# Expert stage of a diffusion step: down weights held in the array, one ring of weight halves, context rows in quarters

## What is computed

```python
aff = softmax(ht @ w_router)              # per request group
gates, idx = top_k(aff.T, cap)            # cap = 128 latent, 32 context
xs = ht[idx]
a = einsum('ecd,edf->ecf', xs, w_gate)    # 16 experts, d = 1024, f = 2816
u = einsum('ecd,edf->ecf', xs, w_up)
y = einsum('ecf,efd->ecd', silu(a) * u, w_down) * gates[..., None]
out = zeros.at[idx].add(y)                # x = x + gate2 * out
```

## Time and profile before

| | us |
|---|---|
| median of three runs | 3479.28 |
| span of the profiled execution | 3480.6 |
| first gate matmul of expert 0 starts | 883.12 |
| last down matmuls of expert 15 start | 3430.77 |
| PE busy | 3166.9 |
| DVE busy | 2532.4 |
| POOL busy | 1483.4 |
| ACT busy | 1278.2 |

### The profile page before, as it was taken

How to read it: one execution, slowest core, us unless ns; L and a number is a source line. 1 busy time by engine, 2 the same in 40 slices (tenths; PEclk the granted TensorE clock), 3 DMA queues, 4 the chain that set the end, 5 groups by cost and what they waited for, 6 DMA issues and landing times. The chain is left out here.

```text
span 3480.6 us, 50738 instructions
## 1 busy us (share of the span) xinstructions
PE 3166.9 (91%) x19191; PEld 2741.1 (79%) x19191; DVE 2532.4 (73%) x3014; ACT 1278.2 (37%) x2046; POOL 1483.4 (43%) x860
## 2 busy tenths in 40 slices
PE   8999989894899999989898999999898989999994
PEld 2699987683788888878787888888787878888883
DVE  2343331225789898988898898989898989889895
ACT  2222221232334434434343344343434343434432
POOL 2233330123345455453545454544535354535443
PEclk9999999996899999999999999999999999999997
DMA  7311102344667676776767676767667576767673
GB/s 303 114 37 36 38 14 74 117 147 151 205 220 247 210 233 214 223 223 212 238 211 240 221 231 217 236 215 234 220 210 245 195 255 205 245 224 226 218 237 134
DMA packets 483305, 668.23 MB, mean 192 GB/s; under 512 B 14689, under 2 KB 418993, under 8 KB 480050
## 3 DMA queue, kind: packets, MB, share of 16 engines
q1 hardware_dynamic: 476978, 644.45, 55.6%
q0 software_dynamic: 6144, 20.98, 2.5%
HBM read 633.39 MB, written 31.98 MB: 191 GB/s over the span
## 5 line engine op out<-in xcount | busy, mean ns | idle before, releaser
L1202 POOL TENSOR_TENSOR wD_lo<-rawW,wD_hi 128x1024 fp32r<-128x1024 f32 x352 | 960.3, 2759 | 1162.7 <-DVE wD_hi L1541 1162.7
L1401 PE MATMUL psU<-X,wU_hi 128*128 128x320 f32 x2816 | 784.7, 360 | 93.1 <-DVE wU_lo L1202 93.1
L1401 PE MATMUL psG<-X,wG_hi 128*128 128x320 f32 x2816 | 760.9, 352 | 38.2 <-issue 35.1
L1202 DVE TENSOR_TENSOR wU_lo<-rawW,wU_hi 128x1024 fp32r<-128x1024 f32 x350 | 741.2, 2125 | 0.0
L1403 PE MATMUL psU<-X,wU_lo 128*128 128x160 f32 x2816 | 685.0, 243 | 0.0
L1403 PE MATMUL psG<-X,wG_lo 128*128 128x160 f32 x2816 | 677.7, 241 | 0.0
L1401 PEld LDWEIGHTS psU<-X,wU_hi 128*128 128x128 f32 x2816 | 552.7, 196 | 98.6 <-DVE wU_lo L1202 51.0
L1401 PEld LDWEIGHTS psG<-X,wG_hi 128*128 128x128 f32 x2816 | 543.7, 193 | 62.9 <-issue 41.7
L1403 PEld LDWEIGHTS psU<-X,wU_lo 128*128 128x128 f32 x2816 | 562.9, 200 | 0.0
L1403 PEld LDWEIGHTS psG<-X,wG_lo 128*128 128x128 f32 x2816 | 552.5, 196 | 6.4
L1202 DVE TENSOR_TENSOR wG_lo<-rawW,wG_hi 128x1024 fp32r<-128x1024 f32 x350 | 454.6, 1336 | 56.9 <-ACT wG_hi L1208 56.9
(11 more groups left out here) (239 smaller groups left out, 4213.0 us busy)
## 6 DMA issues: line engine op xcount, KB each, us to landing
rawW<-in_w_gate SPq DMA_DIRECT2D x176, 1024.0 KB, 7.4
rawW<-in_w_up SPq DMA_DIRECT2D x176, 1024.0 KB, 8.2
rawW<-in_w_down SPq DMA_DIRECT2D x176, 1024.0 KB, 4.9
wm<-in_w_mod SPq DMA_DIRECT2D x24, 1024.0 KB, 5.0
raw<-in_w_in SPq DMA_DIRECT2D x32, 192.0 KB, 2.4
rawc<-catT SPq DMA_DIRECT2D x10, 512.0 KB, 6.0
acc<-x SPq DMA_DIRECT2D x10, 512.0 KB, 2.7
xn<-xn SPq DMA_DIRECT2D x10, 512.0 KB, 4.1
```

Of the source, the lines that this page charges most:

```text
L1202: eng.tensor_tensor(lo, src, hi.bitcast(F32), ALU.subtract).then_inc(f_lo[kind], 1)
L1401: pe.matmul(out[:, f, 0:2 * C], hi, X[:, k, :], start=(k == 0), stop=False, skip_group_check=True)
```

## The change

The stage is written anew; the parts before and after it stay, but for the gate row of routing.

- **Weights.** All weights of an expert are 66 halves of 128x1024: 44 of gate and up, in the order of the steps, then 22 of down. A down half is four blocks of 128x256 out of one of four passes over the 1024 output columns. The halves run through one ring of 11 raw buffers (`RAW`) and one of 6 split buffers (`SPLIT`), whose place goes on over the change of expert. ACT makes every `hi` and DVE every `lo`, four halves ahead of PE in their lists (`AHEAD`); POOL makes none after routing.
- **Down.** It follows after the eleven gate and up steps. The weights are held and the hidden values stream, in pairs of 320 and 160 columns as for gate and up: 4 passes x 22 blocks x 2 = 176 pairs, into `psD0` and `psD1` by turns. The results are columns of tokens. ACT copies a pass's lo columns out, scaled by the gate vector (`y_low`); DVE adds the rest, scaled too (`y_sum`). Ten transposes turn all to rows (`columns_to_rows`), after the up matmuls of the next expert's first step, and ACT copies them out with the token's gate (`y_rows`).
- **Context.** Its 32 rows of 1024 are gathered and scattered as 128 rows of 256. The gathered rows are turned in one place, after the first pass (`rows_to_columns`, ten transposes); ACT and DVE modulate them (`x_modulated`).
- **Routing.** The gate row's operations go; three copies and four scalings of indices come on DVE, and two more halves to split.

The diff, cut to its core (of removed lines, only those that nothing replaces):

```diff
+        HALF = NK // 2 * W_STEP
+        GU_HALVES, HALVES = 4 * STEPS, 6 * STEPS
+        PASSES, FB = 4, FF // P
+        RAW, SPLIT, AHEAD = 11, 6, 4
+        raw = sb("rawW", [P, RAW, HALF])
+        w_hi, w_lo = sb("w_hi", [P, SPLIT, HALF], F32R), sb("w_lo", [P, SPLIT, HALF], F32R)
...
+        def parts(n):
+            if n < GU_HALVES:
+                i, kind, half = n // 4, n // 2 % 2, n % 2
+                return [((wg_, wu_)[kind], 4 * half, 4, i * W_STEP)]
+            t = 4 * (n - GU_HALVES)
+            inside = min(4, FB - t % FB)
+            out = [(wd_, t % FB, inside, t // FB * W_STEP)]
+            return out + ([(wd_, 0, 4 - inside, (t // FB + 1) * W_STEP)] if inside < 4 else [])
...
+        def load(sp, e, n):
+            at = 0
+            for src, row, rows, col in parts(n):
+                dst = raw[:, n % RAW, at * W_STEP:(at + rows) * W_STEP].rearrange("p (k f) -> p k f", k=rows)
+                src = src[:, bass.ds(e, 1), row:row + rows, col:col + W_STEP].rearrange("p e k f -> p (e k) f")
+                sp.dma_start(dst, src).then_inc(f_raw[n % RAW], 16)
+                at += rows
+        def half_hi(act, e, n):
+            act.wait_ge(f_raw[n % RAW], PER_EXPERT[n % RAW] * e + LANDED[n])
+            if not isinstance(e, int) or HALVES * e + n >= SPLIT:
+                act.wait_ge(f_use, HALVES * e + n - SPLIT + 1)
+            act.activation(w_hi[:, n % SPLIT, :], raw[:, n % RAW, :], ACT.Copy).then_inc(f_hi, 1)
+        def half_lo(eng, e, n):
+            eng.wait_ge(f_hi, HALVES * e + n + 1)
+            eng.tensor_tensor(w_lo[:, n % SPLIT, :], raw[:, n % RAW, :], w_hi[:, n % SPLIT, :].bitcast(F32),
+                              ALU.subtract).then_inc(f_lo, 1)
...
-                    dve.tensor_copy(idxf[32:48, CP:2 * CP], idxf[32:48, 0:CP])
-                    dve.tensor_copy(vals[32:48, CP:2 * CP], vals[32:48, 0:CP]).then_inc(e_f, 1)
+                    for j in range(Q4 - 1, 0, -1):
+                        dve.tensor_copy(vals[32:48, j * CP:(j + 1) * CP], vals[32:48, 0:CP])
+                        dve.tensor_scalar(idxf[32:48, j * CP:(j + 1) * CP], idxf[32:48, 0:CP], float(Q4), float(j),
+                                          ALU.mult, ALU.add)
+                    dve.tensor_scalar(idxf[32:48, 0:CP], idxf[32:48, 0:CP], float(Q4), None, ALU.mult).then_inc(e_f, 1)
...
+                        for n in range(RAW if first else 0, HALVES):
+                            sp.wait_ge(f_lo, HALVES * e + n - RAW + 1)
+                            load(sp, e, n)
...
+                    def down_tile(n, q):
+                        t = 4 * (n - GU_HALVES) + q
+                        f, out = t % FB, psD[t // FB % 2]
+                        hi, lo = (w[:, n % SPLIT, :].rearrange("p (k f) -> p k f", k=4) for w in (w_hi, w_lo))
+                        for b in range(2):
+                            pe.matmul(out[:, b, 0:2 * C], hi[:, q, b * P:(b + 1) * P], hid[:, f, :],
+                                      start=(f == 0), stop=False, skip_group_check=True)
+                            mm = pe.matmul(out[:, b, 0:C], lo[:, q, b * P:(b + 1) * P], hid[:, f, 0:C],
+                                           start=False, stop=(f == FB - 1), skip_group_check=True)
+                        return mm
...
+                    def rows_to_columns(e):
+                        pe.wait_ge(f_got, 32 * (e + 1))
+                        lat = psG[:].rearrange("p b (k c) -> p (b k) c", c=P)
                         for k in range(NK):
+                            pe.transpose(lat[:, k, :], xg[0][:, k * P:(k + 1) * P], ident[:])
+                        for b in range(2):
+                            mm = pe.transpose(psU[:, 0, b * P:(b + 1) * P], xg[1][:, b * P:(b + 1) * P], ident[:])
+                        mm.then_inc(f_xt, 1)
+                    def columns_to_rows(e):
+                        pe.wait_ge(f_yt, 2 * PASSES * (e + 1))
+                        lat = psD[0][:].rearrange("p b (k c) -> p (b k) c", c=P)
+                        for k in range(NK):
+                            pe.transpose(lat[:, k, :], yT[:, k, :], ident[:])
+                        for b in range(2):
+                            mm = pe.transpose(psD[1][:, 0, b * P:(b + 1) * P], yTc[:, b, :, :].rearrange("p j c -> p (j c)"),
+                                              ident[:])
+                        mm.then_inc(f_tr, 1)
+                    rows_to_columns(0)
...
+                            gate_or_up(psG, e, i, 0)
                             if i:
+                                pe.wait_ge(f_ua, s)
+                            gate_or_up(psU, e, i, 1)
+                            if i == 0 and not first:
+                                columns_to_rows(e - 1)
+                        for n in range(GU_HALVES, HALVES):
+                            pe.wait_ge(f_lo, HALVES * e + n + 1)
+                            for q in range(4):
+                                t = 4 * (n - GU_HALVES) + q
+                                j, f = t // FB, t % FB
+                                if j == 0 and f % 2 == 0:
+                                    pe.wait_ge(f_hl, STEPS * e + f // 2 + 1)
+                                if f == 0 and j == 0 and not first:
+                                    pe.wait_ge(f_y, e)
+                                if f == 0 and j >= 2:
+                                    pe.wait_ge(f_yt, 2 * (PASSES * e + j - 1))
+                                mm = down_tile(n, q)
+                                if j == 0 and f == FB - 1 and not last:
+                                    pe.wait_ge(f_ua, STEPS * (e + 1))
+                                    rows_to_columns(e + 1)
+                            mm.then_inc(f_use, 1)
                     experts(pe, body)
+                    columns_to_rows(E - 1)
...
+                    def y_low(e, j):
+                        act.wait_ge(f_use, HALVES * e + GU_HALVES + (FB * (j + 1) - 1) // 4 + 1)
+                        if not isinstance(e, int) or PASSES * e + j:
+                            act.wait_ge(f_yt, 2 * (PASSES * e + j))
+                        for b in range(2):
+                            for r, a, z in ((0, 0, CS), (1, CS, C)):
+                                op = act.activation(yl[:, b, a:z], psD[j % 2][:, b, C + a:C + z], ACT.Copy,
+                                                    scale=modT[:, 5, 2 * j + b, r:r + 1])
+                            op.then_inc(f_yl, 1)
+                    def y_rows(e):
+                        act.wait_ge(f_tr, e + 1)
+                        act.wait_ge(f_si, e + 1)
+                        act.activation(ys[0][:], psD[0][:].rearrange("p b c -> p (b c)"), ACT.Copy, scale=gc[:, 0:1])
+                        act.activation(ys[1][:], psD[1][:, 0, 0:D // Q4], ACT.Copy, scale=gc[:, 1:2]).then_inc(f_y, 1)
...
+                            n = 4 * i + AHEAD
+                            if i:
+                                after_up(e, i - 1)
+                            elif not first:
+                                y_low(e - 1, PASSES - 1)
+                            if not (first and i == 0):
+                                ahead_hi(e, n, last)
+                            if i:
+                                hidden_hi(e, i - 1)
+                            if not (first and i == 0):
+                                ahead_hi(e, n + 1, last)
+                            if i == 1 and not first:
+                                y_rows(e - 1)
+                            after_gate(e, i)
+                            ahead_hi(e, n + 2, last)
+                            gate_on(e, i)
+                            ahead_hi(e, n + 3, last)
+                        for q in range(STEPS):
+                            n = GU_HALVES + 2 * q + AHEAD
+                            if q == 0:
+                                after_up(e, STEPS - 1)
+                            if q in (3, 6, 9):
+                                y_low(e, q // 3 - 1)
+                            ahead_hi(e, n, last)
+                            if q == 0:
+                                hidden_hi(e, STEPS - 1)
+                            if q == 3 and not last:
+                                x_modulated(e + 1)
+                            if q == 4 and not last:
                                 x_hi(e + 1)
+                            ahead_hi(e, n + 1, last)
...
+                    def y_sum(e, j):
+                        for b in range(2):
+                            dve.wait_ge(f_yl, 2 * (PASSES * e + j) + b + 1)
+                            for r, a, z, out in ((0, 0, CS, yT[:, 2 * j + b, :]), (1, CS, C, yTc[:, b, j, :])):
+                                op = dve.scalar_tensor_tensor(out, psD[j % 2][:, b, a:z],
+                                                              modT[:, 5, 2 * j + b, r:r + 1], yl[:, b, a:z],
+                                                              ALU.mult, ALU.add)
```

(48 more changed lines are left out.)

394 lines of the change are left out of this document (139 added, 255 removed).

## The result

The changed kernel takes 3209.53 us (median of four runs, 3209.04 to 3209.74), the one before 3479.98 beside it (3478.57 to 3482.09). The ratio is 0.9221, 95% interval 0.9208 to 0.9234. The forecast was 3215.

What follows compares the result with a forecast made beforehand. PE was taken to pace the stage, a tenth of it waiting. Start 883.1, pairs 2185.9, transposes 39.3, branches 55.9, clock 1.6, end 49.2 and routing 1 gave 3216, less 1.3 to the median: 3215 us, range 3185 to 3240.

Steps and rivals of the forecast that it cites:

- PE paces the stage, and what it waits for decides: Expert stage: PE sets the pace and a tenth of each expert is waiting; 160.65 us an expert falls to 143.
- The waits, 9.9 us an expert, are POOL's doing: PE's waits on `lo` and `hid`, 6.1 + 0.6, go with two clock falls of 1.62 once POOL stops subtracting.
- DVE and ACT have room: Splitting: DVE needs 113 us an expert, ACT 101 to 118, within PE's 143; PE has over 5 us in hand.
- C: Rival: one gap an expert stays where ACT's and DVE's lists meet a change or pass end; 70 us, 3285; chance 0.13.
- E: Rival: DVE becomes the bound, its 66 `lo` staying slow at 2.125 us; 3700 us; chance 0.04.
- Down, 22 x 2.07 = 45.5: Down matmuls: 176 pairs at gate's 0.259 us take 45.5 an expert instead of 52.1, so 6.6 less.
- Transposes, 1.31 a group: Two groups of ten an expert replace eight times 0.38: 2.6 us instead of 3.0, clock staying at 1.00.
- rival B: The clock falls at each group of transposes as at a gap; 49 us more, 3264; chance 0.07.
- Change of expert, 4.3 at 13 branches: PE's gap of 2.7 us plus a clock fall of 1.62 stays at each of 13 branches back, 55.9 in all.
- Rival A: The gap at the change of expert goes, since a steady ring frees the full DMA engines; 56 less, 3159; chance 0.12.
- Loads are free: Weight loads: 34.6 MB an expert at 242 GB/s cost nothing, with about 20 us of cover for each load.
- D: Rival: the loads set the pace at no more than 225 GB/s, 153.8 us an expert; 3393 us; chance 0.05.

Runs made afterwards that it cites:

- ahead2: The changed kernel with ACT and DVE making the halves two ahead of PE in their lists, not four; 3250.73 us, ratio 0.9334.
- transposes5: The changed kernel with eight of each group's ten transposes done five times over, 42 in a row instead of 10; 3317.30 us, ratio 0.9521.
- pool_junk: The changed kernel with POOL also subtracting 22 halves an expert in a buffer of its own that nobody reads; 3205.84 us, ratio 0.9209.
- before_dve_lo: The kernel before with the down weights' `lo` halves moved from POOL to the end of each step of DVE's list; 3411.75 us, ratio 0.9793.
- lo_on_pool: The changed kernel with every second `lo` half moved from DVE to POOL, 33 of 66 an expert; 3278.32 us, ratio 0.9411.

## Why the prediction was right, step by step

**PE paces the stage, and what it waits for decides.** Right: an expert takes 142.9 us from gather to gather (1736.63 to 1879.53), 143 had been said, and the earlier trace rows gave 160.65.

**The waits, 9.9 us an expert, are POOL's doing.** Right, and now shown by itself: taking POOL's arithmetic out of the old stage gave 3483.5 - 3311.4 = 172 us within its set, where 16 x 9.9 = 158 had been said. 107 of it came with the subtractions, 66 with the context operations. I had spoken of the second as four more operations in an expert's first steps; per us of POOL's time they were the dearer ones: 14 us an expert (the rows above and one of 3.35) cost 4.1, and 22 subtractions of 2.76, 61 us, cost 6.7. The changed kernel would take 0.9221 x 3483.5 = 3212 in that set; the 99 us that are left are put down to down and the transposes (said: 106 and 6), which no run takes apart.

**DVE and ACT have room.** Right, with too high estimates: 105 us an expert and 92, where 113 and 101 to 118 had been worked out. The cover of four halves was called over 5 us in the steps; there even two halves are enough (ahead2). Rivals C and E fall with the waits and the busy row above: no step waits for DVE, which is busy 61%. What I took as the tightest place of the cover, behind the first pass, is one of the two at which it decides. The cover and the fast DVE each hide much of what the other would cost: 22 subtractions on POOL are nearly free behind it, half of the `lo` cost 69.

**Down, 22 x 2.07 = 45.5.** Right: 138.52 us without a gap, less two groups of transposes at 1.01, leave 136.50 for 528 pairs, 0.2585 each. The analogy with gate held; why it holds (0.146 and 0.113) the sum did not need.

**Transposes, 1.31 a group.** Mis-sized: 1.01. The 1.31 of the earlier trace rows is the length of a record that covers ten, and a record outlasts the start of what comes next; from start to start is the price, as I had done for pairs. That explains only a part, since the matmul behind those ten in the kernel before,

```profile
54.48 7.03 PE L221 MATMUL mod<-wm,cond 128*2 128x512 f32 x16
```

starts 54.48 - 53.24 = 1.24 behind their first. The other 0.23 is the place: ten transposes cost more between the first stage's matmuls than between the pairs of this one, and why no run shows. 30 x 0.30 = 9 us is more than the whole miss of 5. The clock stayed up, so rival B falls, and transposes5 shows it for groups four times as long; the rule of the Trainium skill's page "TensorE: Matmul & The Clock Gate", section "Part 4: PE-mode transpose", that went with B did not show here.

**Change of expert, 4.3 at 13 branches.** Right in sum: 36.1 us of gaps and 19.1 of clock are 55.2, and 55.9 had been said. That a gap costs 1.62 of clock held for most gaps only: read pair by pair, three of the 13 lost 0.1, eight 1.3 to 1.7 and two some 3, so that their mean of 1.5 comes near 1.62 is in part luck. Rival A fell in the trace of after: the ring runs on, the DMA share ahead of the change is 0.88 (1735 to 1740) and not 1.08, and the gap is the same. I had left it because nothing touched it; that it belongs to the branch was a guess, now shown.

**Loads are free.** Right: ACT's waits in the stage are for PE and DVE, none for loads, at 252 GB/s (D would have had 225).

**Sum.** PE starts at 885.0 (said: 884.1 with routing), its last pair ends at 3160.3 (3166.8), and the span 47.6 behind that (49.2). 16 x 528 x 0.2585 + 30 x 1.01 + 55.2 + 1.6 = 2271, measured 2275. The span came out 8 under the 3216 of the sum, the median 5 under the forecast: the step from span to median, taken as -1.3, was +1.6. So the 5 is the transposes' 9, set off in part by terms that were too low.

## What to carry to other kernels

Look in the trace at the least, median and most of one operation on an engine: where they differ by three, something beside it may be holding it up, and work that was moved to a "free" engine may be what makes the bound wait. Price work on PE from start to start, never by the length of a record. A branch back in the list of the engine that paces the kernel can cost it a pause each time: here 13 branches were worth 58 us, and only PE's list needed to be straight.

## What the runs showed of the hardware

POOL does not slow all of DVE. `ga` and `ua`, with one operand in PSUM, took at most 0.493 us in the kernel before and in pool_junk alike; `lo`, `hf`, `hid`, `X` and the second `xm`, with both in SBUF, took several times as long (`lo` up to 4.101 in pool_junk; in the rows above `xm` 0.42 out of `psU` and 1.67 out of `xm`). That `xm` began at 1705.31 and ended at 1706.98, 0.28 behind the end of POOL's operation: it did not run slowly but stood behind it. The `lo` ahead of it, which began before POOL's operation, kept its 1.23. It is so for all `lo` of pool_junk that met one subtraction: 193 began after it and ended about 1.08 us behind its end, with lengths mostly from 1.68 to 2.93; 288 began before it, kept 1.21 to 1.23, and the subtraction ended 1.75 to 1.78 behind theirs. Both lengths behind POOL's end are 0.14 less than what the operation takes alone (0.42 and 1.22). Who starts first goes first, and the other waits. The Trainium skill's page "SBUF — State Buffer", section "SBUF: two separate sides", says so: an exclusive lock for the whole instruction, against DVE operations with two SBUF inputs; the trace agrees, by these figures.

A wait can pay for a part of itself: in before_dve_lo 4.8 us of waiting hid a gap of 2.6 with its fall of the clock. A wait that is taken away should be priced with what it covers.

The clock does not fall at every pause, nor for the same time. Behind a gap of 0.90 (ahead2) 23 pairs ran at 0.26, and behind one of 2.58 in the changed kernel they ran at 0.48 after the first three. But gaps of one length do not agree: behind one of 2.60, at 2312.20, no pair but the first was slower than 0.27, and in lo_on_pool ten waits of 2.1 were followed by a fall and five were not. Two windows of the changed kernel, the first behind its gap of 3.54, show the two levels, 0.50 (1.2 GHz) and 1.00 (2.4 GHz):

```profile
2168.01:2173.50 5.49, 5.49 (x23) 5.49 (x24) 0.91 (x1) 0.00 (x0) 0.00 (x0) 0.50 0.73 232
2312.20:2315.80 3.60, 3.25 (x23) 3.14 (x24) 1.85 (x2) 0.40 (x1) 0.00 (x0) 1.00 0.76 243
```

So a price per gap is an average over many, not what one gap costs.
